# Splitting a weight block's product into a pass over its high parts and a pass over its low parts

## What is computed

```python
merged = (g_attn * jnp.einsum("bte,ed->btd", attn, w_o_attn[l])
          + g_rnn * jnp.einsum("bte,ed->btd", rnn, w_o_rnn[l])
          + g_conv * jnp.einsum("bte,ed->btd", cnv, w_o_conv[l]))
h = h + jnp.einsum("btd,de->bte", merged, w_out[l])
f = rms_norm(h, ffn_norm_g[l])
a = silu(f @ w_ffn_gate[l]) * (f @ w_ffn_up[l])
h = h + a @ w_ffn_down[l]
```

## Time and profile before

| quantity | value |
|---|---|
| median of three runs | 3548.93 us |
| profiled execution | 3545.81 us |
| its span on the core | 3544.0 us |
| PE matmul busy | 3427.8 us (97%) |
| DVE busy | 2337.7 us (66%) |
| POOL busy | 2041.8 us (58%) |
| ACT busy | 992.4 us (28%) |
| POOL idle before line 495 | 1431.1 us, of it 1408.5 us waiting for PE |

### The profile page before, as it was taken

One profiled execution on the slowest core, in us unless ns is written; L12 is line 12 of the kernel. 1 busy time (PEld: TensorE's weight loads), 2 busy tenths in 40 slices (PEclk: granted clock), 3 DMA queues, 4 the chain that ended last, 5 costly groups with the idle time before them and its releaser, 6 DMA issues.

```text
span 3544.0 us, 49543 instructions
## 1 busy us (share of the span) xinstructions
PE 3427.8 (97%) x19986; PEld 2978.8 (84%) x19986; DVE 2337.7 (66%) x2945; ACT 992.4 (28%) x1717; POOL 2041.8 (58%) x1100
## 2 busy tenths in 40 slices
PE   8999899999999999999999999999999999999998
PEld 7899789999999879977778778878887875788886
DVE  7787898867832578888887863386326765643425
ACT  5406442312110241654231110111103444322201
POOL 4355334656666545533566766677665662466664
PEclk9999999999999999999999999999999999999999
DMA  4122112222323322211223433343335341222332
GB/s 143 60 90 78 48 49 66 84 86 94 127 90 100 113 66 90 80 54 58 83 84 109 147 125 102 103 142 128 101 107 191 145 158 60 95 95 95 105 104 77
DMA packets 96897, 348.29 MB, mean 98 GB/s; under 512 B 10848, under 2 KB 13152, under 8 KB 93664
## 3 DMA queue, kind: packets, MB, share of 16 engines
q1 hardware_dynamic: 80064, 289.44, 25.2%
q10 hardware_dynamic: 16672, 56.70, 4.2%
HBM read 322.32 MB, written 23.79 MB: 98 GB/s over the span
## 4 chain that ended last, share of the span: by engine, by line
PE 75%; DVE 19%; ACT 3%; issue 2%; DMA 1%; POOL 0%; ACTq 0%; DVEq 0%; POOLq 0%
PE acc L524 23%; PE acc L525 22%; PE acc L527 22%; DVE cu L2093 3%; PE acc L788 1%; DVE ptmp L2296 1%; PE aux L840 1%; DVE fpr L1829 1%; PE acc L869 1%; DVE pap L2296 1%; PE aux L715 1%; DVE pcp L2296 1%; DVE mtmp L1880 1%; PE aux L695 1%; PE aux L759 1%
## 5 line engine op out<-in xcount | busy, mean ns | idle before, releaser
L495 POOL TENSOR_SCALAR whi<-raw 128x1024 fp32r<-128x1024 f32 x548 | 625.7, 1142 | 1431.1 <-PE acc L527 1408.5
L497 POOL TENSOR_TENSOR wlo<-raw,whi 128x1024 fp32r<-128x1024 f32 x548 | 1416.2, 2584 | 45.7
L524 PE MATMUL acc<-nhi_s,whi 128*128 128x512 f32 x1568 | 618.7, 395 | 18.7 <-DVE fpr L1826 5.5
L525 PE MATMUL acc<-nlo_s,whi 128*128 128x512 f32 x1568 | 611.4, 390 | 0.0
L527 PE MATMUL acc<-nhi_s,wlo 128*128 128x512 f32 x1568 | 611.3, 390 | 0.0
L524 PE MATMUL acc<-bhi,whi 128*128 128x264 f32 (+1 forms) x1864 | 555.2, 314 | 12.7 <-ACT tqg L1160 5.7
L525 PE MATMUL acc<-blo,whi 128*128 128x264 f32 (+1 forms) x1864 | 541.3, 307 | 0.0
L527 PE MATMUL acc<-bhi,wlo 128*128 128x264 f32 (+1 forms) x1864 | 446.6, 306 | 0.0
L524 PEld LDWEIGHTS acc<-bhi,whi 128*128 128x128 f32 x1864 | 353.5, 190 | 43.6 <-issue 10.2
L524 PEld LDWEIGHTS acc<-nhi_s,whi 128*128 128x128 f32 x1568 | 294.9, 188 | 90.1 <-issue 12.8
L525 PEld LDWEIGHTS acc<-blo,whi 128*128 128x128 f32 x1864 | 353.3, 190 | 14.9
(11 more groups left out here) (421 smaller groups left out, 5820.3 us busy)
## 6 DMA issues: line engine op xcount, KB each, us to landing
raw<-in_w SPq DMA_DIRECT2D x548, 512.0 KB, 3.3
kept_cp<-pcp ACTq DMA_DIRECT2D x4, 1280.0 KB, 6.8
cp<-kept_cp ACTq DMA_DIRECT2D x4, 1280.0 KB, 9.9
kept_ap<-pap ACTq DMA_DIRECT2D x4, 1024.0 KB, 6.1
kept_cs<-pcs ACTq DMA_DIRECT2D x4, 1024.0 KB, 6.5
ap__152<-kept_ap ACTq DMA_DIRECT2D x4, 1024.0 KB, 7.1
cs__163<-kept_cs ACTq DMA_DIRECT2D x4, 1024.0 KB, 6.9
merge_gates<-gout ACTq DMA_DIRECT2D x16, 256.0 KB, 2.2
```

The source lines that it names most:

```text
L495: pool.tensor_scalar(hi, w, 1.0, 0.0, ALU.mult, ALU.add).then_inc(sem("w_hi"), 1)
L497: pool.tensor_tensor(lo, w, hi.bitcast(F32), ALU.subtract).then_inc(sem("w_split"), 1)
L524: pe.matmul(acc[s][:, f, 0:TH], hi, xh[:, f * TH:(f + 1) * TH], start=a, stop=False)
L525: pe.matmul(acc[s][:, f, 0:TH], hi, xl[:, f * TH:(f + 1) * TH], start=False, stop=False)
```

## The change

PE no longer takes the three products of a weight tile together in a plain tile. `high_products` runs all high x high and high x rest products of the block and then adds one to `pe_block`; `low_products` runs all rest x high products and adds another one. PE waits for `w_hi` ahead of the first and for `w_split` ahead of the second. `pe_block` therefore counts two for a block. All other forms of a tile wait as before and add two at their end. ACT and DVE wait for `2 * b`, the same moment as before. GpSimd waits for `2 * b - 3` (the high pass of block b-2 is over) ahead of `whi`, and for `2 * b - 2` (its low pass is over) ahead of `wlo`.

```diff
                 pool.tensor_scalar(hi, w, 1.0, 0.0, ALU.mult, ALU.add).then_inc(sem("w_hi"), 1)
                 pool.wait_ge(sem("w_hi"), b + 1)
+                if b >= 2:
+                    pool.wait_ge(pe_block, 2 * b - 2)
                 pool.tensor_tensor(lo, w, hi.bitcast(F32), ALU.subtract).then_inc(sem("w_split"), 1)
...
                 if b >= 2:
-                    pool.wait_ge(pe_block, b - 1)
+                    pool.wait_ge(pe_block, 2 * b - 3)
...
+            def high_products(s, slot, j0, nk, rhs, T, first):
+
+                TH = T // 2 if T > 512 else T
+                for j in range(nk):
+                    hi = whi[:, slot, j * P:(j + 1) * P]
+                    xh, xl = rhs(j0 + j)
+                    for f in range(T // TH):
+                        pe.matmul(acc[s][:, f, 0:TH], hi, xh[:, f * TH:(f + 1) * TH], start=first and j == 0, stop=False)
+                        m = pe.matmul(acc[s][:, f, 0:TH], hi, xl[:, f * TH:(f + 1) * TH], start=False, stop=False)
+                return m
+
+            def low_products(s, slot, j0, nk, rhs, T, last):
+
+                TH = T // 2 if T > 512 else T
+                for j in range(nk):
+                    lo = wlo[:, slot, j * P:(j + 1) * P]
+                    xh = rhs(j0 + j)[0]
+                    for f in range(T // TH):
+                        m = pe.matmul(acc[s][:, f, 0:TH], lo, xh[:, f * TH:(f + 1) * TH], start=False,
+                                      stop=last and j == nk - 1)
+                return m
...
                 for c in range(ph.per):
                     b = ph.block(i) + c
-                    pe.wait_ge(sem("w_split"), b + 1 + m * (step * ph.per))
                     k0, kk = cuts(nk, ph.per)[c]
                     if each is None:
-                        products(s, b % 2, k0, kk, rhs, T, c == 0, c == ph.per - 1).then_inc(pe_block, 1)
+                        pe.wait_ge(sem("w_hi"), b + 1 + m * (step * ph.per))
+                        high_products(s, b % 2, k0, kk, rhs, T, c == 0).then_inc(pe_block, 1)
+                        pe.wait_ge(sem("w_split"), b + 1 + m * (step * ph.per))
+                        low_products(s, b % 2, k0, kk, rhs, T, c == ph.per - 1).then_inc(pe_block, 1)
                         continue
+                    pe.wait_ge(sem("w_split"), b + 1 + m * (step * ph.per))
...
-                    p.then_inc(pe_block, 1)
+                    p.then_inc(pe_block, 2)
...
             def block_done(b):
-                dve.wait_ge(pe_block, b)
+                dve.wait_ge(pe_block, b * 2)
```

More of the change, by code:

```diff
@@ L1025, in _ @@
                     m = short((2 * i + e) % 4, b % 2, 4 * e, 4, R(attn_hi, attn_lo, S))
-                m.then_inc(pe_block, 1)
+                m.then_inc(pe_block, 2)
             for j in range(2):
@@ L1063, in block_done @@
             def block_done(b):
-                act.wait_ge(pe_block, b)
+                act.wait_ge(pe_block, b * 2)
             def std(i):
```

2 lines of the change are left out of this document (1 added, 1 removed).

## The result

The changed kernel takes 3567.4 us (median of 4 runs, 3565.92 to 3572.4), the one before in the same comparison 3548.3 us (4 runs, 3543.93 to 3549.46): ratio 1.0053, 95% interval 1.0037 to 1.0069. The forecast was 3545 us with a range of 3538 to 3553; the time lies 22 us above the forecast and outside the range.

What follows compares the result with a forecast made beforehand. PE was taken as the bound, its matmuls in flight 97% of the span, with only idle time behind POOL to win: 5.5 - 1.1 - 0.4 = 4.0 us off 3548.9 gives 3544.9, say 3545 us, range 3538 to 3553.

Steps and rivals of the forecast that it cites:

- What bounds the kernel: PE, with matmuls in flight 97% of the span; only its idle time behind POOL can be won, 4.0 us behind `wlo`.
- The POOL stalls: PE's nine waits for `wlo` in `up1`, `up2` and the SSM all go, worth at most 5.5 us.
- What stands in their place: DVE is next to be late: 1.1 us given back in `up1` and `up2`, 0.4 us swallowed in the SSM.
- The added wait and the order on TensorE: 455 added waits, added increments and the new matmul order on PE cost 0; bound at most 4.5 us.
- The rule on increments: Increments on matmul completion serialize, about 26 ns each: 455 more cost 11.8 us, time about 3557 us; chance 1 in 100.
- What moves for DVE and ACT: POOL meets DVE at other moments; 20 PE waits at plain tile ends shift about 1.3 us either way: 0, spread 3 us.
- A: The port DVE and POOL share is full in `up1`, `up2`; only the SSM's 1.5 us are won: 3547.5 us, chance 0.16.
- B: Slower: `wlo` directly behind each tile's end holds DVE's first two-SBUF-input operation 2.4 instead of 1.06 us: 3559 us, chance 0.11.
- C: Faster: `wlo` ends 1.15 us earlier, so DVE chains at tile ends shorten; 10 us won, 3539 us, chance 0.13.
- The tell-tales: Signs to check: waits for `tqg`, `cgate`, `cstat`, `rb` (19.2 us together) changing over some 5 us would prove the forecast wrong.

Runs made afterwards that it cites:

- Halving `wlo`: From the third block on, GpSimd makes the low part of 512 of 1024 columns only: 3483.33 us in the kernel before, 3482.92 us in the changed kernel.
- Order alone: Kernel before, with TensorE running high pass then low pass behind one wait and with one release of both parts at the end: 3546.56 us, ratio 0.9998.
- The `up` runs: Changed form in up0 to up3 only, old form elsewhere: parts released separately 3566.28 us, together 3549.9, `whi` released late 3552.73, together with `wlo` delayed 3557.78.
- the late `whi`: Changed kernel, but in all plain blocks `whi` is given back five weight tiles ahead of the low pass's end: 3563.28 us, ratio 1.0046.
- the gap in the old phase: Changed TensorE order, both parts given back at the block's end, but `wlo` waits until TensorE is four weight tiles into the next block: 3592.88 us.
- the joint release: Changed kernel with its two TensorE waits, but both parts given back together at the end of the low pass: 3556.73 us, ratio 1.0026.
- the narrow selection: Changed form only in vki, qi, kq, conv, mg_att and out, old form elsewhere: 3544.06 us, ratio 0.999 against the kernel before.

## Why the prediction was wrong

**What bounds the kernel**: right as far as it went. TensorE is the engine that sets the end, and only its idle time can be won. But the waits were read as belonging to whoever released them. Halving `wlo` brings 66 us where the row for it says 4.0: GpSimd's price was inside the VectorE and ScalarE entries.

**The POOL stalls**: right. No wait for `wlo` is left. The view files 2.1 us in three waits under `whi`, against the mark of no such wait "of more than 0.1 us"; by their rows `fpr` ended them as much. The idle time of line 495 and of line 499 is about 1 us each (1.17 and 0.82 in the rows above), as was said.

**What stands in their place**: right in kind, wrong in size. VectorE was named as "the next to be late", with 1.1 us given back (bounds 0 and 3.6). The `fpr` waits grew by 10.4 us, with those filed under `whi` by 12.5, outside the bounds, since those took VectorE's round as fixed and only let it begin late. The round itself got longer: 8.7 to 10.2 us for four operations of the table and 0.75 to 2.34 for `alo_s`, in the round shown.

**The added wait and the order on TensorE**: right. Order alone measures 0.9998 (0.9989 to 1.0008), and the rows at the turn from high to low pass in after keep their distance, 0.23 us, to be held against the earlier trace rows:

```profile
1710.43 0.39 PE L540 MATMUL acc<-blo,whi 128*128 128x512 f32 x1
1710.66 1.56 PE L550 MATMUL acc<-bhi,wlo 128*128 128x512 f32 x6
```

The rule on increments from the Trainium skill ("TensorE: Matmul & The Clock Gate", section "The cost: per-tile semaphore tail"), given 1 in 100, is not seen: the matmul at 1710.43 is the one that increments, and the next starts 0.23 us behind it. The halved runs leave no room for 11.8 us from it either: with half of `wlo`, the kernel after has 455 more increments and is 0.4 us faster.

**The step that failed: "What moves for DVE and ACT".** It said "POOL's work per block stays 3.5 us, and DVE gets the same room", took 0 and a spread of 3 us. The first half is true (GpSimd's instructions are the same, its busy time even 21 us less), the second is not. Room in two pieces is not the same room: in the round shown, with the pieces apart, four operations of VectorE met four pieces, where one of the four had met none, and `alo_s` met a `wlo` at the tile's end. A wait that the step let move by 1.3 us either way went from 1.24 to 4.12, another from 0.67 to 4.12. The `up` runs show it for the stages: same pieces, same order on TensorE, released separately +17.2 us in up0 to up2 and 42 us more of VectorE, released together +0.7 us and 0. The second half of the same step, signs that cancel at tile ends, was closer: `conv_gate` lost 5.3 us, `mg_att0` and `proj1` won 1.4 and 3.2.

**The rivals.** A had the right engine, and its tell-tale, `fpr` above 6.1 us, came true; but it priced a full port at no gain (3547.5), not at a loss. B, slower, had the right sign. Its mechanism, `wlo` first behind the tile's end, does exist. In `mg_att0` before and after (the same operation, the second behind a tile's end; the first reads PSUM):

```profile
644.06 0.85 DVE L2106 TENSOR_TENSOR merged<-merged,mt 128x528 f32<-128x528 f32 x1
```

```profile
640.87 2.27 DVE L2133 TENSOR_TENSOR merged<-merged,mt 128x528 f32<-128x528 f32 x1
...
640.18 2.39 POOL L499 TENSOR_TENSOR wlo<-raw,whi 128x1024 fp32r<-128x1024 f32 x1 [0.94 <-PE acc L550]
```

There slack swallows it (the stage even wins 1.4 us). It costs where TensorE waits for the chain. For `conv_gate`, 5 us in after and 16 in the run with the late `whi`, that is argued: those runs have `wlo` first, while the gap in the old phase costs 1.4 us there and the joint release nothing. What part of the 19 us is B's is not separated from the gap's. C, the gain, is seen in single stages; chosen for them, the narrow selection has a span 5.5 us shorter than before, and by its ratio it is 3.5 us faster.

**The tell-tales**: `tqg`, `cgate`, `cstat` and `rb` together went from 19.2 to 25.1 us, past the "some 5 us" that the prediction named as its undoing.

What is not settled: how the 19 us divide between the gap and `wlo` first at a tile's end (without the gap, with the late `whi`, the whole kernel still loses 15.6 us, the `up` stages alone +6.1), what `up2` loses by, and how much of the state-space stage's loss another phase of the same chain would give back. The 5.4 us there are shown for one arrangement, by its rows.

## What to carry to other kernels

Where two engines exclude each other, the price of one is hidden in the waits for the other: do not read it from the row with its name, but leave half of its work out once and see what the kernel gains. When such an engine's job is cut in two, the other engine's operations meet it at other moments: in the `up` stages here a gap of about 0.8 us between the pieces cost VectorE time, in the `down` and `conv_out` stages it saved some, so look at the stages where the bottleneck waits for that engine. Where a wait has two releasers that end close together, look at both: the view names one. And before a small wait is taken away, look at what it holds back: here its removal put GpSimd beside the last link of VectorE's chain.

## What the runs showed of the hardware

The exclusion is by whole instructions and reaches further than the operations with two inputs that the prediction had in mind. L2459 has one SBUF input, and beside `wlo` takes 2.71 us, where L2453, of the same form, took 0.69 at 1940.89 with GpSimd idle; GpSimd's one-input `whi` holds VectorE too (0.09 us of the kernel per microsecond, against 0.10 for the subtraction). The Trainium skill, "SBUF — State Buffer", section "SBUF: two separate sides", has this as an exclusive lock that whoever starts first keeps for the whole instruction. The trace agrees in kind: 2.03 us for L2456, started 0.10 us behind a GpSimd start, against 1.22 us for the like operation L2430 started at an idle GpSimd.

A VectorE that is never alone is a good deal slower than its instructions: 359 of its 2338 busy us went away with 640 us of GpSimd's.

A long idle time of TensorE can be paid twice. Behind 4.12 us of waiting the granted clock of the next 4.4 us was 0.50, the 1.2 GHz level, and the matmuls stood 0.43 us apart in place of 0.23; behind one of 2.05 us it stayed 1.00. Over the whole change longer matmuls are 7.8 us on top of 12.3 us of idle time.
